# The last pair of experts as code of its own behind the loop: residual and first expert's share summed in PSUM ahead, decode rows in two strips

## What is computed

```python
x = x + gt2 * moe_ffn(h, w_router, b_router, w_up, b_up, w_down, b_down)
...
def expert(acc, e):
    wu, bu, wd, bd, cw = e
    y = clamped_swiglu(t @ wu + bu) @ wd + bd
    return acc + cw[:, None].astype(t.dtype) * y, None
...
rmsnorm(x, g_final)            # y = x * rsqrt(mean(x*x) + EPS) * g
```

## Time and profile before

| | |
|---|---|
| median of 3 runs | 1220.29 us |
| profiled execution, time | 1219.88 us |
| profiled execution, span | 1218.0 us |
| TensorE matmul busy | 1139.1 us (94%) |
| VectorE busy | 350.4 us (29%) |
| ScalarE busy | 174.8 us (14%) |
| GpSimd busy | 64.4 us (5%) |
| chain that ended last | PE 68%, DMA 29%, VectorE 1%, ScalarE 1%, issue 1% |
| DMA moved | 462.05 MB, mean 379 GB/s |

### The profile page before, as it was taken

The page is one execution under the profiler, slowest core; times in us unless marked ns, Lnnn a source line. Parts: engine busy times, 40 slices in busy tenths (PEclk is TensorE's granted clock), DMA queues, the critical chain, the costliest instruction groups (busy, mean ns, idle before and its releaser), DMA issues.

```text
span 1218.0 us, 14326 instructions
## 1 busy us (share of the span) xinstructions
PE 1139.1 (94%) x5548; PEld 469.9 (39%) x5548; DVE 350.4 (29%) x739; ACT 174.8 (14%) x321; POOL 64.4 (5%) x98
## 2 busy tenths in 40 slices
PE   6899998989999998989898989898989898989896
PEld 3778756843332333323232323232323232323231
DVE  2545466242222132222222121212121212222224
ACT  2331250220110101010101010101010101010102
POOL 3400000200000000000000000000000000000000
PEclk9999998989999999999999999999999999999999
DMA  9961289569999999999999999999999999999991
GB/s 364 362 237 69 96 362 353 191 245 393 429 430 431 429 430 430 431 430 432 432 432 431 430 430 430 431 430 430 431 430 430 431 431 430 430 432 431 430 399 48
DMA packets 46336, 462.05 MB, mean 379 GB/s; under 512 B 7007, under 2 KB 8223, under 8 KB 18488
## 3 DMA queue, kind: packets, MB, share of 16 engines
q1 hardware_dynamic: 38850, 444.16, 86.8%
q0 software_dynamic: 6208, 13.64, 3.2%
q10 hardware_dynamic: 1256, 3.95, 0.9%
HBM read 461.33 MB, written 5.78 MB: 384 GB/s over the span
## 4 chain that ended last, share of the span: by engine, by line
PE 68%; DMA 29%; DVE 1%; ACT 1%; issue 1%; SPq 0%; ACTq 0%; POOL 0%; DVEq 0%; POOLq 0%
PE bank L1434 34%; DMA ring<-in_w_up 24%; PE bank L1328 6%; PE bank L1427 5%; PE bank L1455 4%; PE bank L821 3%; PE bank L922 3%; PE bank L899 2%; PE bank L1242 2%; DMA arena<-in_w_down 2%; PE bank L995 1%; PE bank L1334 1%; DMA ring<-in_w_in 1%; PE bank L979 1%; DMA ring<-in_w_out 1%; PE bank L845 1%
## 5 line engine op out<-in xcount | busy, mean ns | idle before, releaser
L1434 PE MATMUL bank<-ring,arena 128*64 128x512 f32 x1536 | 363.9, 605 | 18.1 <-DMA ring<-in_w_up 14.1
L1434 PEld LDWEIGHTS bank<-ring,arena 128*64 128x64 f32 x1536 | 98.3, 137 | 260.3 <-issue 215.0
L1455 PE MATMUL bank<-arena 128*64 128x512 f32 x512 | 116.1, 596 | 19.8 <-DMA arena<-in_w_down 19.8
L1455 PE MATMUL bank<-ring,arena 128*64 128x512 f32 x512 | 116.3, 596 | 0.0
L1434 PE MATMUL bank<-arena 128*64 128x512 f32 x512 | 116.1, 595 | 0.0
L1967 DVE TENSOR_SCALAR arena<-bank 128x256 f32<-128x256 f32 x64 | 24.2, 420 | 290.6 <-PE bank L1434 290.6
L1328 PE MATMUL bank<-arena,mods 128*128 128x512 f32 (+2 forms) x204 | 94.4, 629 | 0.0
L785 ACT ACTIVATE arena<-arena 128x512 f32<-128x512 f32 x32 | 20.2, 631 | 502.7 <-DVE arena L1967 502.7
L1957 DVE TENSOR_TENSOR x<-x,bank 128x512 f32<-128x512 f32 x64 | 44.0, 688 | 148.3 <-PE bank L1328 148.3
L1984 DVE COPY arena<-bank 64x512 f32<-64x512 f32 x32 | 22.0, 688 | 185.2 <-PE bank L1455 185.2
L1455 PEld LDWEIGHTS bank<-arena 128*64 128x64 f32 x512 | 37.0, 136 | 98.2 <-issue 72.2
(11 more groups left out here) (323 smaller groups left out, 826.7 us busy)
## 6 DMA issues: line engine op xcount, KB each, us to landing
ring<-in_w_up SPq DMA_DIRECT2D x96, 2048.0 KB, 24.4
arena<-in_w_up SPq DMA_DIRECT2D x32, 2048.0 KB, 25.1
ring<-in_w_down SPq DMA_DIRECT2D x32, 2048.0 KB, 22.5
arena<-in_w_down SPq DMA_DIRECT2D x32, 2048.0 KB, 23.9
ring<-in_w_ada SPq DMA_DIRECT2D x24, 1024.0 KB, 10.7
ring<-in_w_in SPq DMA_DIRECT2D x5, 2048.0 KB, 18.7
arena<-in_state_hgrn POOLq DMA_DIRECT2D x8, 256.0 KB, 10.4
ring<-in_w_out SPq DMA_DIRECT2D x8, 256.0 KB, 5.5
```

The costliest lines, as they stand in the source:

```text
L1434: mm = pe.matmul(B[2 * e + c % 2][64 * a:64 * a + 64, :], lhsT=xTe[:, k, 64 * e:64 * e + 64], rhs=big(n)[:, CH * r + 512 * c:CH * r + 512 ...
L1455: mm = pe.matmul(B[4 + e][64 * a:64 * a + 64, :], lhsT=gT[e].rearrange("p (j a t) -> p j a t", j=4, a=2)[:, k % 4, k // 4, :], rhs=big(n). ...
```

## The change

The loops run one iteration less: `npass` now holds `passes * PAIRS - 1`, read as `ahead`. The loop's body is a function `pair_steps(it, last)`, called once in the loop and once behind it with `last` set. In the last pair:

- no rows are searched, gathered or transposed for a next pair, no next bias is loaded;
- TensorE adds the residual `x` of the prompt tokens into banks 0 to 3 by identity matmuls (four in all), two behind `turn_g(1)` in the first down projection and two in the second one ahead of k-step 2;
- the weighted sum is made for each expert by itself, over its 64 slots: the first expert's ahead of k-step 5 of the second down projection, the second's behind the last k-step, the decode rows between the two token blocks;
- VectorE multiplies banks 4 and 5 by the gate straight into `ysg` (`half_gated`), ScalarE copies both halves into `ysb` for the decode rows (`y_kept`, `y_crossed`);
- the final norm of the prompt tokens reads banks 0 to 3; VectorE's residual additions are gone;
- the decode rows lie in two strips (partitions 0 to 7 and 32 to 39, 512 columns each) of 64-partition tiles: `gate_st`, `g_st`, `wst` (residual and earlier pairs' share, made during the second down projection), `vst`. Their square sums are added across the strips by a matmul with the new constant `strips`; the store has two parts.

Ahead of the loop, the gating waits for `gate_full` = 16 (`gate2` alone). The strips of the gate (`gate_s_full`) are waited for in the last pair. In the diff, the streams follow in the order SP, POOL, ScalarE, TensorE, VectorE. The constant `diag`, equal to `ident`, is gone, so the constant table has 96 columns less.

```diff
-            with sp.Fori(0, total) as it:
+            def other_chunks(it):
                 for c in range(BIGS, PER):
                     sp.wait_ge(chunks_used, it * PER + (PRE + c - BIGS + 1))
                     expert_chunk(c, it % PAIRS)
-                with sp.If(it < total - 1):
-                    for c in range(BIGS):
-                        sp.wait_ge(chunks_used, it * PER + (PRE + PER + c - BIGS + 1))
-                        expert_chunk(c, (it + 1) % PAIRS)
+            with sp.Fori(0, ahead) as it:
+                other_chunks(it)
+                for c in range(BIGS):
+                    sp.wait_ge(chunks_used, it * PER + (PRE + PER + c - BIGS + 1))
+                    expert_chunk(c, (it + 1) % PAIRS)
+            other_chunks(ahead)
...
             pool.dma_start(gate2, wide(mod_dram[0:1, :], 0, P)).then_inc(sem("gate_full"), 16)
-            pool.dma_start(gate2s[0:NB, :], mod_dram[1:1 + NB, :]).then_inc(sem("gate_full"), 16)
+            pool.memset(gate_st, 0.0).then_inc(sem("gate_s_cleared"), 1)
+            pool.wait_ge(sem("gate_s_cleared"), 1)
+            for a in range(2):
+                pool.dma_start(gate_st[32 * a:32 * a + NB, :], mod_dram[1:1 + NB, 512 * a:512 * (a + 1)]).then_inc(sem("gate_s_full"), 16)
...
+            pool.wait_ge(sem("xT_made"), 2)
+            for a in range(2):
+                pool.dma_start(g_st[32 * a:32 * a + NB, :], wide(A["g_final"].rearrange("(a n) -> a n", a=1)[:, 512 * a:512 * (a + 1)], 0, NB)).then_inc(sem("g_fin_full"), 16)
...
+                    if last:
+                        other = slice(64 * (1 - e), 64 * (1 - e) + 64)
+                        act.wait_ge(sem("half_gated"), 2 * e + 1)
+                        act.activation(ysb[r, 1 - e, :], B[4 + e][other, :], ACT.Copy).then_inc(sem("y_crossed"), 1)
...
+                def residual(t):
+                    for a in range(2):
+                        pe.matmul(B[2 * t + a][:, :], lhsT=ident, rhs=x[:, t, 512 * a:512 * (a + 1)], start=True, stop=False,
+                                  skip_group_check=True)
+                def combine_tokens(e, t):
+                    r = slice(64 * e, 64 * e + 64)
+                    for a in range(2):
+                        pe.wait_ge(sem("half_gated"), 2 * e + 2 if a == e else 2 * e + 1)
+                        mm = pe.matmul(B[2 * t + a][:, :], lhsT=Wc[r, P * t:P * (t + 1)], rhs=ysg[r, a, :], start=False, stop=bool(e),
+                                       skip_group_check=True)
+                        if e:
+                            mm.then_inc(sem("x2_made"), 1)
+                def combine_decode(e):
+                    r = slice(64 * e, 64 * e + 64)
+                    pe.wait_ge(sem("y_kept"), e + 1)
+                    pe.wait_ge(sem("y_crossed"), e + 1)
+                    for a in range(2):
+                        mm = pe.matmul(B[6][32 * a:32 * a + 32, :], lhsT=Wc[r, S:S + 32], rhs=ysb[r, a, :], start=(e == 0), stop=bool(e),
+                                       skip_group_check=True)
+                    if e:
+                        mm.then_inc(sem("decode_made"), 1)
...
-                            turn_rows(it * 16 + 16)
+                            if not last:
+                                turn_rows(it * 16 + 16)
                             turn_g(1)
+                            if last:
+                                residual(0)
+                        if last and e and k == 2:
+                            pe.wait_ge(sem("u_read"), it * 2 + 3)
+                            residual(1)
+                        if last and e and k == 5:
+                            combine_decode(0)
+                            for t in range(2):
+                                combine_tokens(0, t)
...
+                if last:
+                    combine_tokens(1, 0)
+                    combine_decode(1)
+                    combine_tokens(1, 1)
+            with pe.Fori(0, ahead) as it:
+                pair_steps(it, False)
+            pair_steps(ahead, True)
+            pe.wait_ge(sem("sums"), 1)
             for a in range(2):
+                mm = pe.matmul(B[4][32 * a:32 * a + 32, 0:1], lhsT=C("strips", slice(0, 64)), rhs=ssum3[0:64, :], start=True, stop=True,
+                               skip_group_check=True)
+            mm.then_inc(sem("v_mean"), 1)
...
-            dve.wait_ge(sem("gate_full"), 32)
+            dve.wait_ge(sem("gate_full"), 16)
...
+                    for e in range(2):
+                        dve.wait_ge(chunks_used, it * PER + (PRE + 2 * UPS + DOWNS * (e + 1)))
+                        other, own = slice(64 * (1 - e), 64 * (1 - e) + 64), slice(64 * e, 64 * e + 64)
+                        dve.tensor_tensor(ysg[own, 1 - e, :], B[4 + e][other, :], gate2[other, 512 * (1 - e):512 * (2 - e)], ALU.mult).then_inc(sem("half_gated"), 1)
+                        dve.wait_ge(sem("y_kept"), e + 1)
+                        dve.tensor_tensor(ysg[own, e, :], B[4 + e][own, :], gate2[own, 512 * e:512 * (e + 1)], ALU.mult).then_inc(sem("half_gated"), 1)
...
             half_mean_of(0)
+            dve.wait_ge(sem("decode_made"), 1)
+            dve.wait_ge(sem("w_ready"), 1)
+            link(dve.tensor_tensor(vst[0:64, :], B[6][0:64, :], gate_st[0:64, :], ALU.mult))
+            dve.tensor_tensor(vst[0:64, :], vst[0:64, :], wst[0:64, :], ALU.add).then_inc(sem("v_ready"), 1)
+            final_norm(0)
             half_mean_of(1)
-            final_norm(0)
             final_norm(1)
```

More of the change, by code:

```diff
@@ L76 @@
 _at = 0
-for _name, _n in (("ident", P), ("ones", P), ("incl", P), ("after", P), ("before", P), ("diag", P), ("levels", 7 * 64),
+for _name, _n in (("ident", P), ("ones", P), ("incl", P), ("after", P), ("before", P), ("levels", 7 * 64),
                   ("window", 2 * P), ("turn", P), ("cos", NTOK), ("sin", NTOK), ("slots", SLOTS), ("iota", E), ("tok", 3),
-                  ("same", NB), ("heads", NB * HH), ("spread", 64)):
+                  ("same", NB), ("heads", NB * HH), ("spread", 64), ("strips", 32)):
     _COLS[_name] = (_at, _at + _n)
@@ L125, in constants @@
     put("heads", same[:, :, None] & (r[:, None, None] // 32 == np.arange(HH)[None, None, :]))
+    put("strips", r[:, None] % 32 == np.arange(32)[None, :])
     put("spread", np.repeat(np.eye(NB), HEADS, 1), NB)
@@ L258, in hybrid_layer @@
         moe_s = at(26736, 512)
-        junk_s = at(23152, D)
-        gate2, gate2s = at(27248, D), at(28272, D)
+        junk_s = at(23664, 512)
+        gate2, gate_st = at(27248, D), at(28272, 512)
+        g_st = at(22128, 512)
+        wst = at(22640, 512)
+        vst = at(23152, 512)
         G = mods[:, :, :].rearrange("p q c -> p (q c)")[:, 0:3 * P].rearrange("p (t e s) -> p t e s", t=3, e=2)
@@ L781, in _, with pair_steps @@
             count_from_one(act, "y_copied_a", "gT_copied")
-            with act.Fori(0, total) as it:
+            def pair_steps(it, last):
                 for e in range(2):
@@ L788, in _ @@
                         act.activation(Wc[:, 0:NTOK], B[4][:, 0:NTOK], ACT.Copy).then_inc(sem("wc_copied"), 1)
-                    if e:
+                    if e and not last:
                         copy_rows(it * 2 + 4)
@@ L1370, in _, with pair_steps @@
             count_from_one(pe, "gT_made")
-            with pe.Fori(0, total) as it:
+            def pair_steps(it, last):
                 def chunk_landed(c):
@@ L1442, in _ @@
                         pe.wait_ge(sem("wc_copied"), it + 2)
-                    else:
+                    elif not last:
                         pe.wait_ge(sem("idx_ready"), it + 1)
@@ L1940, in _, with pair_steps @@
             count_from_one(dve, "g_ready", "u_read", "sum_added", "y_copied_d")
-            with dve.Fori(0, total) as it:
+            def pair_steps(it, last):
                 pair = bass.ds((it % PAIRS) * 2, 2)
@@ L1945, in _ @@
                 dve.tensor_tensor(GW, G, wide(wd[:, :, pair].unsqueeze(3), 3, SLOTS), ALU.mult).then_inc(sem("gw_built"), 1)
-                dve.tensor_scalar(rk1[:, :, pair], rk1[:, :, pair], -float(SLOTS), None, ALU.add).then_inc(sem("rank_lowered"), 1)
-                dve.wait_ge(sem("rank_lowered"), it + 1)
-                build_rows(after).then_inc(sem("g_built"), 1)
+                if not last:
+                    dve.tensor_scalar(rk1[:, :, pair], rk1[:, :, pair], -float(SLOTS), None, ALU.add).then_inc(sem("rank_lowered"), 1)
+                    dve.wait_ge(sem("rank_lowered"), it + 1)
+                    build_rows(after).then_inc(sem("g_built"), 1)
                 dve.wait_ge(sem("sum_added"), it * 5 + 1)
@@ L1995, in half_mean_of @@
+            with dve.Fori(0, ahead) as it:
+                pair_steps(it, False)
+            pair_steps(ahead, True)
             def half_mean_of(t):
```

113 lines of the change are left out of this document (47 added, 66 removed).

## The result

The changed kernel takes 1227.36 us, the median of 7 runs (1224.63 to 1228.71), where the kernel before takes 1220.29 (1219.09 to 1224.06, 7 runs beside it). The ratio is 1.0052, 95% interval 1.0036 to 1.0068: slower by some 7 us, by more than 0.2%, and above the forecast range. The profiled execution took 1228.48 us, its span is 1226.8, 8.8 more than before.

A forecast was written before the change was run, and what follows sets the result against it. It took the late loop to wait for DMA weight transfers, anchored to TensorE's first chunks. Start -0.8 and end +1.35 summed to +0.55: 1220.8 us beside the median of 1220.29, range 1217.4 to 1223.4.

The forecast's parts named there:

- part 2 of the prediction: Ahead of the loop: POOL's added memset and transfers are covered, and the smaller constant table gives at most 0.1 us; taken 0.
- Part 3: The loop for all but the last pair: same work issued, DMA sets the late pace, no gap at the seam; 0.
- the rivals: Other outcomes: clock back 0.15, early work nearly free 0.08, costlier shape changes or late code, slower, 0.17.
- The gating's wait: Ahead of the loop: gating waits for `gate2` alone, TensorE starts at 257.2 instead of 258.0 behind ScalarE's copy; -0.8 us.
- The clock: Loop's start: about 1.7 us of TensorE idle remains, so the half clock stays and the first 16 records keep 6.41 us.
- the rival of the returning clock: Loop's start: less idle brings the clock back, the 6.41 us shrink by 1.2 to 3.0; time 1217.8 to 1219.6; chance 0.15.
- The last pair: Last pair's own code: TensorE's added matmuls end the last down projection at 1206.3 where before it ended at 1199.94.
- Changes of array shape: Last pair: some nine changes at about 0.15 us each; rival of 0.5 each adds 3.1 us, 0.17 together with late code.
- The new code: Loop's seam: fetching the last pair's separate code is mostly covered and costs nothing; as a rival, a few hundredths of the chance.
- Behind the loop: Last k-step to span's end: gating straight from PSUM, no VectorE residual additions, decode rows last; 13.0 us instead of 18.1.
- +1.35: Span's end: the way behind the sum is 5.0 us shorter, but TensorE's last down projection comes 6.4 us late.
- +0.55: Whole kernel: the sum of -0.8 at the loop's start and +1.35 at the end.

The follow-up runs named there:

- third run: The kernel before with only the shorter constant table (`diag` replaced by `ident`, `strips` added and not used): 1228.92 us, ratio 1.0081.
- fifth: The kernel before with two small tiles (`idx`, `top8i`) moved in front of the weight ring, table as before: 1228.81 us, ratio 1.0077.

## Why the prediction was wrong

The step that failed is the one in part 2 of the prediction: "The smaller constant table (96 columns, 48 KB less) is worth at most 0.1 us of the start's DMA; taken 0". It counted the table's bytes and not what its length does to the addresses behind it. The short table costs 8.7 us by itself (third run) and 9.3 by addresses alone (fifth). Part 3 took the loop as unchanged because its instructions are; it is, but not the addresses that they write to. The earlier trace rows had said that the late loop goes through the weight transfer, so whatever slows a transfer is paid there in full. None of the rivals had a mechanism that slows the DMA.

How a misplaced ring costs time is shown down to the single row and no further: rows of 16 KB take 616 ns in the mean in place of 611.5. The sum, 0.53 us of 59.75 per pair, is 0.9%; laid on the ring's 8 chunks alone it is 0.066 per chunk, 1.3% of the 59.75 / 12 = 4.98 that a chunk takes. The Trainium skill, DMA: Bandwidth & Descriptors, section "How a descriptor splits into AXI transactions", says that a transaction has to begin on a multiple of 256 bytes, and that a descriptor which doesn't begin there starts with one from the boundary below, whose first bytes are fetched for nothing. By that a row of 16 KB is 65 transactions in place of 64, an estimate of 1.6% whatever the distance. The section tells it of what is read; here it is the side written. That 32, 64, 96 and 128 bytes cost the same agrees. That 97 to 98% of all rows took 611 ns while the arena's buffers were 96 bytes off, and that with the ring 32 off rows into the arena were longer too, doesn't agree, and the measurement decides. So the ring's place is shown as the cause, and the mechanism behind it stays open.

The other steps, against the traces:

- *The gating's wait, -0.8: right.* In the run with this wait alone it measured -0.87, with ScalarE's copy next, as argued. That is one pair of profiles, and the starts spread by more. Measured from the end of that copy, the seven profiles with the new wait begin 0.23 or 0.24 behind it, the seven with the old one 0.39 to 1.71 behind it, 0.98 in the mean: some 0.7 us. In the changed kernel's own profile the start is later (260.46), because the copy and all in front of it are. VectorE's gating in its timeline still waits for a transfer, but it starts earlier than the copy:

```profile
259.35 1.29 DVE L1986 TENSOR_TENSOR arena<-arena 128x512 f32<-128x512 f32 x2 [2.84 <-DMA arena<-mod_rows]
```

 The first matmul starts between 255.4 and 260.9 over the profiles, one each. The part that the ring's place has in this (other weights pass through the ring before the loop) isn't separated from the spread.
- *The clock: it is still lost, but it costs less than the sum had it.* The windows of the changed kernel show half the clock still from 262 to 263. But its first 16 records took 5.23, and the sum left them at 6.41; the rival of the returning clock had 1.2 less. With the new wait TensorE idles 1.74 or 1.75 ahead of them, and all seven profiles have 5.13 to 5.30. With the old wait three profiles have 5.06 to 5.08, behind 1.90 to 2.09 of idle, and four have 5.92 to 6.47, behind 2.50 to 3.22. By these fourteen profiles the new wait avoids a loss of about 1 us that the old one has in some executions; what that is worth in the median isn't shown.

```profile
262.00:263.00 1.00, 1.00 (x4) 0.24 (x2) 0.00 (x0) 0.00 (x0) 0.00 (x0) 0.50 0.00 0
```

- *The last pair: right.* From the second chunk's use to the last k-step's end the sum gave 1206.3 - 1186.62 = 19.7; the chain above has 1214.96 - 1195.20 = 19.8. There is no wait for the last chunk, as said. A residual took 1.72 and 1.91, the first share 0.98 + 3.63 = 4.6 (4.75 in the sum). Changes of array shape cost what was taken, not more. The tokens' 8 records over 64 rows took 0.45 each: by the row of the bias, and not by the factor of up to 2 that the Trainium skill, TensorEngine Tiling (Array Packing), "Theoretical Speedup", gives for short contractions.
- *The new code: right.* The instruction queue moved two packets more. At the seam TensorE waits 1.24 us for weights, as it did a pair earlier inside the loop (1.23), and no more. The lines are the queue, then the first weight matmuls of the pair ahead and of the last one:

```profile
q8 instruction: 17, 0.28, 0.1%
...
1091.08 3.65 PE L1479 MATMUL bank<-ring,arena 128*64 128x512 f32 x16 [1.23 <-DMA ring<-in_w_up]
...
1151.13 3.65 PE L1479 MATMUL bank<-ring,arena 128*64 128x512 f32 x16 [1.24 <-DMA ring<-in_w_up]
```

- *Behind the loop: right in order, 1.2 us too long.* From the last k-step to the span's end the sum gave 1219.35 - 1206.3 = 13.05; measured 1226.8 - 1214.96 = 11.8. The decode rows are last, as said. The timeline has the decode gating at 1218.73, 3.8 behind the k-step (4.05), the decode square at 1221.94 already beside the second norm's chain, and the root behind the small matmuls at 1222.97, 8.0 behind the k-step where the sum had about 9.2; the rest is in the landing of the store, 1.6 in place of 1.85.

```profile
1218.73 0.68 DVE L2074 TENSOR_TENSOR arena<-bank,arena 64x512 f32<-64x512 f32 x1
...
1221.94 0.61 ACT L828 ACTIVATE arena<-arena 64x512 f32<-64x512 f32 x1
...
1222.70 0.23 PE L1527 MATMUL bank<-small,const 64*32 64x1 f32 x4 [2.11 <-ACT arena L828]
1222.97 0.26 ACT L830 ACTIVATE small<-bank,small 64x1 f32<-64x1 f32 x1 [0.33 <-PE bank L1527]
...
1224.55 0.67 SPq L472 DMA_DIRECT2D out_ys<-x  x2
```

So the end is +0.2 and not +1.35, and with the start -0.9 the code is worth -0.7 in the traces, before the clock. The two timed versions with the old addresses give -1.2 (0.9977 to 1.0002) and -1.5 (0.9978 to 0.9999) by their ratios, with which that agrees. So without the table the time would have lain in the stated range, but the sum, +0.55, had the wrong sign: the end was 1.1 too long in it, and the clock's part was left out. The prediction's chances don't add up either: its parts put 0.74 on no change that can be told and 0.09 on faster, where it states 0.62 and 0.20, and the overlong tail that it names for the rest has no chance of its own. Table (+8.7 to +9.3) and code together come to 7.2 to 8.1; the ratios of the two timings of the change, 1.0052 and 1.0057, give 6.3 and 7.0, with intervals of some 2 us to either side.

## What to carry to other kernels

A constant's length, or any tile allocated ahead of a streamed buffer, is an edit to that buffer's address: work out the address before and after, and where the stream sets the pace, keep it on a multiple of 256 bytes. If the DMA share is full in two profiles and the GB/s differ, ask where the bytes land before asking what was reordered. And to see what a change of code is worth, give it the addresses of the kernel before.

## What was not expected of the hardware

A stream of 2 MB transfers in rows of 16 KB went from 431 to 427 GB/s, at a DMA share of 1.01 in both, when the buffers of eight of its twelve chunks began off a multiple of 256 bytes in SBUF, by as little as 32 bytes. A kernel bound by that stream took 0.7 to 0.8% more. The single rows took 616 ns in the mean in place of 611.5. It isn't a price of each row's own start: the two other buffers lay 96 bytes off in the kernel before too, and there 98% of all rows took 611 ns. No run here says why.
